# Second pair of each feed-forward entry on two other banks; conv layer norm, merged tiles and heads' taps in another order around the weight splits

## What is computed

```
mod = silu(c) @ ada_w + ada_b                     # 9 vectors of 1024: shift, scale, gate x3
h = modulate(rms_norm(x)); g, u = split(h @ w_in) # w_in 1024 x 5632
x += 0.5 * g1 * ((silu(g) * u) @ w_out)           # feed-forward 1, inner width 2816
h = modulate(rms_norm(x)); q,k,v,u,gates = split(h @ w_mix_in)   # 1024 x 7168
y_attn = rms_norm(diff_attention(q, k, v)) @ w_attn_branch       # 8 heads, 2 maps each
z = depthwise_conv31(a * sigmoid(g))              # causal, over tokens, from u
y_conv = silu(layer_norm(z)) @ w_conv_branch
x += g2 * ((sigmoid(ga) * y_attn + sigmoid(gb) * y_conv) @ w_mix_out)
x += 0.5 * g3 * feed_forward_2(modulate(rms_norm(x)))
```

## Time and profile before

| | |
|---|---|
| plain runs | 2654.38 us (2653.51 to 2656.37) |
| the profiled execution | 2656.59 us |
| its span, first to last instruction | 2654.8 us |
| mean granted TensorE clock | 0.992 |
| TensorE matmul / weight load busy | 2571.9 / 2064.5 us |
| VectorE / ScalarE / GpSimd busy | 1672.3 / 972.7 / 102.4 us |
| moved by DMA | 311.93 MB, mean 117 GB/s |

### The profile page before, as it was taken

One profiled execution on the slowest core, in us unless ns is written; L12 is line 12 of the kernel. 1 busy time (PEld: TensorE's weight loads), 2 busy tenths in 40 slices (PEclk: granted clock), 3 DMA queues, 4 the chain that ended last, 5 costly groups with the idle time before them and its releaser, 6 DMA issues.

```text
span 2654.8 us, 34931 instructions
## 1 busy us (share of the span) xinstructions
PE 2571.9 (97%) x11578; PEld 2064.5 (78%) x11578; DVE 1672.3 (63%) x2449; ACT 972.7 (37%) x1637; POOL 102.4 (4%) x163
## 2 busy tenths in 40 slices
PE   4899999999999999999999999999999999999998
PEld 2688888777777887888878888877777778788886
DVE  3655576789888666543365555679888866644333
ACT  2422222554454433222232222244554453432222
POOL 0000001000000000000000000101000000000000
PEclk9899999999999999999999999999999999999998
DMA  6355456222223344543325555632222333333332
GB/s 225 114 157 158 150 182 220 77 81 82 79 83 88 92 126 118 153 125 92 102 84 157 156 154 164 222 99 84 79 83 79 91 92 90 87 95 95 95 98 92
DMA packets 469951, 311.93 MB, mean 117 GB/s; under 512 B 11047, under 2 KB 447529, under 8 KB 468872
## 3 DMA queue, kind: packets, MB, share of 16 engines
q1 hardware_dynamic: 445260, 227.69, 29.3%
q0 software_dynamic: 19584, 75.51, 8.4%
q10 hardware_dynamic: 5052, 8.02, 1.0%
HBM read 306.13 MB, written 5.05 MB: 117 GB/s over the span
## 4 chain that ended last, share of the span: by engine, by line
PE 79%; DVE 8%; issue 8%; ACT 3%; ACTq 1%; DVEq 0%
PE bank L1211 24%; PE bank L1213 23%; PE bank L1212 23%; DVE conv_part L1004 3%; PE bank L1406 1%; ACT w_hi L394 1%; ACTq L446 1%; PE bank L1237 1%; DVE w_lo L683 1%; PE bank L1232 1%; PE bank L1233 1%; PE bank L1283 1%; DVE scaled L705 1%; PE bank L1377 1%; PE bank L1310 1%
## 5 line engine op out<-in xcount | busy, mean ns | idle before, releaser
L683 DVE TENSOR_TENSOR w_lo<-w_raw,w_hi 128x1024 fp32r<-128x1024 f32 (+1 forms) x434 | 522.4, 1204 | 626.4 <-ACT w_hi L394 625.7
L1211 PE MATMUL bank<-h_hi,w_hi 128*128 128x512 f32 x2112 | 842.1, 399 | 14.9 <-DVE scaled L908 10.3
L1213 PE MATMUL bank<-h_hi,w_lo 128*128 128x512 f32 x2112 | 826.1, 391 | 0.0
L1212 PE MATMUL bank<-h_lo,w_hi 128*128 128x512 f32 x2112 | 824.6, 390 | 0.0
L394 ACT ACTIVATE w_hi<-w_raw 128x1024 fp32r<-128x1024 f32 (+1 forms) x434 | 451.6, 1041 | 862.9 <-PE bank L1213 851.5
L1211 PEld LDWEIGHTS bank<-h_hi,w_hi 128*128 128x128 f32 x2112 | 398.2, 189 | 109.0 <-issue 28.0
L1213 PEld LDWEIGHTS bank<-h_hi,w_lo 128*128 128x128 f32 x2112 | 397.7, 188 | 85.0
L1212 PEld LDWEIGHTS bank<-h_lo,w_hi 128*128 128x128 f32 x2112 | 398.7, 189 | 78.6 <-issue 0.5
L1004 DVE SCALAR_TENSOR_TENSOR conv_part<-glu,conv_taps,conv_part 128x512 f32<-128x512 f32 x464 | 318.6, 743 | 0.0
L1211 PE MATMUL bank<-s_hi,w_hi 128*128 128x512 f32 x704 | 274.6, 390 | 0.0
L1213 PE MATMUL bank<-s_hi,w_lo 128*128 128x512 f32 x704 | 274.0, 389 | 0.0
(11 more groups left out here) (182 smaller groups left out, 2647.1 us busy)
## 6 DMA issues: line engine op xcount, KB each, us to landing
w_raw<-in_ffn_w_in SPq DMA_DIRECT2D x176, 512.0 KB, 3.8
ada_raw<-in_ada_w POOLq DMA_DIRECT2D x128, 512.0 KB, 4.8
w_raw<-in_w_mix_in SPq DMA_DIRECT2D x112, 512.0 KB, 3.7
w_raw<-in_ffn_w_out SPq DMA_DIRECT2D x64, 512.0 KB, 3.8
w_raw<-in_ffn_w_out SPq DMA_DIRECT2D x32, 384.0 KB, 3.4
w_raw<-in_w_mix_out SPq DMA_DIRECT2D x18, 512.0 KB, 3.8
ada_first<-in_ada_w POOLq DMA_DIRECT2D x8, 1024.0 KB, 24.4
w_raw<-in_w_attn_branch SPq DMA_DIRECT2D x16, 512.0 KB, 3.8
```

The costliest lines, as they stand in the source:

```text
L683: dve.tensor_tensor(wlo[slot][:, 0:n, :], raw[slot][:, 0:n, :], whi[slot][:, 0:n, :].bitcast(F32), ALU.subtract).then_inc(w_lo[slot], 1)
L1211: pe.matmul(acc, wh, hi[:, k0 + k, :], start=first and k == 0, stop=False)
L1212: pe.matmul(acc, wh, lo[:, k0 + k, :], start=False, stop=False)
L1213: mm = pe.matmul(acc, wl, hi[:, k0 + k, :], start=False, stop=last and k == n - 1)
```

## The change

Three parts.

**Entries.** The second pair of each feed-forward entry (tile 1) accumulates into banks TP[0] and TP[1] (banks 4 and 5, used by the heads for turned matrices) and no longer waits for a reader of its bank; ScalarE and VectorE read tile 1 there. TensorE's tile 2, now written out ahead of the loop (`PEELED` 3), needs one read of G less.

**Heads and order.** The taps between the splits are dealt out differently. In "ab" and "brb" VectorE's tile work comes ahead of the split of the next weights and waits for the product itself.

**Layer norm.** The mean moves to block 1 of the next slab, the variance to block 1 of slot 0 of the second ab pair. Squares, centring and sums are spread differently over the slots; the root stands behind one more split on ScalarE, the reciprocal one slot later on VectorE.

```diff
-PEELED = 2
+PEELED = 3
-LN_SQUARES = {(2, 1): (0, 1), (3, 0): (2, 3), (3, 1): (4, 5, 6, 7)}
+LN_SQUARES = {(3, 0): (0, 1, 2, 3), (3, 1): (4, 5), (4, 0): (6, 7)}
...
-                    act.activation(T[0][:, :], G[0][:, :], ACT.Tanh, scale=0.5).then_inc(sem("g_tanh"), 1)
+                    act.activation(T[0][:, :], gate[:, :], ACT.Tanh, scale=0.5).then_inc(sem("g_tanh"), 1)
...
-                ffn_tile(1, False)
+                ffn_tile(1, False, TP[0])
...
                     conv_norm(j, 0)
+                    w_hi_part(p + 1, 1)
                     if j == LN_VAR:
                         root(l * AUXN + AUX_VAR, l * UNITS + UNIT_LN)
-                    w_hi_part(p + 1, 1)
...
-                assert PEELED == 2
-                ffn_tile(1, split=False)
+                assert PEELED == 3
+                ffn_tile(1, split=False, banks=TP)
+                ffn_tile(2)
...
-                    conv(8, 17)
+                    conv(8, 16)
                     if not first:
                         w_lo_part(p + 1, 1)
-                    conv(17, 22)
+                    conv(16, 21)
                     w_lo_part(p + 2, 0)
-                    conv(22, 25)
+                    conv(21, 23)
                     dve.wait_ge(sem("bt_in"), (hh + 1) * 16)
                     scores(3)
                     if not first:
                         head_lo(hh - 1, tile(AOLO2, h - 1), tile(AOHI2, h - 1))
-                    conv(25, 26)
+                    conv(23, 26)
                     scores(2)
...
                     for t in range(2):
-                        w_lo_part(p + 1, t)
                         if j >= KT // 2:
                             n = 2 * (j - KT // 2) + t
+                            dve.wait_ge(w_used[t], p + 1)
                             dve.scalar_tensor_tensor(out=GA[:, n, :], in0=GA[:, n, :], scalar=1.0, in1=G[t][:, :],
                                                      op0=ALU.add, op1=ALU.mult).then_inc(acc_read[t], 1)
+                        w_lo_part(p + 1, t)
...
                             add_ln(3)
-                        if (j, t) == (LN_MEAN + 1, 1):
                             centre(4)
                             centre(5)
+                        if (j, t) == (LN_MEAN + 1, 1):
                             add_ln(4)
                             centre(6)
                             add_ln(5)
                             centre(7)
+                        if (j, t) == (LN_VAR, 0):
                             add_ln(6)
                             add_ln(7)
-                        if (j, t) == (LN_VAR, 0):
+                        if (j, t) == (LN_VAR, 1):
                             reciprocal(l * AUXN + AUX_VAR, l * RSN + RS_VAR)
...
-                        w_lo_part(l * PAIRS + PAIR0["brb"] + i + 1, t)
+                        dve.wait_ge(w_used[t], l * PAIRS + PAIR0["brb"] + i + 1)
...
                         dve.tensor_tensor(F[t][:, :], tile(GA2, j), T[t][:, :], ALU.add).then_inc(sem("merged"), 1)
+                        w_lo_part(l * PAIRS + PAIR0["brb"] + i + 1, t)
                         dve.wait_ge(sem("m_hi"), l * KT + j + 1)
...
-                        pe.wait_ge(acc_read[slot], use)
+                        if banks is G:
+                            pe.wait_ge(acc_read[slot], use)
...
+                    wh, wl, acc = whi[slot][:, n, :], wlo[slot][:, n, :], banks[slot][:, :]
...
-            two_slabs(pair + 1, use + 1, lambda j: pe.wait_ge(sem("unit_lo"), l * UNITS + UNIT_NORM[k] + j + 1))
+            two_slabs(pair + 1, use + 1, lambda j: pe.wait_ge(sem("unit_lo"), l * UNITS + UNIT_NORM[k] + j + 1),
+                      banks=G if name == "mix" else TP)
...
-                def ffn_tile(i):
+                def ffn_tile(i, reads=0):
                     p = l * PAIRS + PAIR0[n_in] + i
-                    u = l * USES + USE0[n_in] + i
+                    u = l * USES + USE0[n_in] + i - reads
...
                 entry(l, 2 * w, n_in)
+                ffn_tile(2, reads=1)
...
-                branch("gb", LN_MEAN + 1, HHI, HLO, ({7: conv_mean}, {}))
+                branch("gb", LN_MEAN + 1, HHI, HLO, ({}, {1: conv_mean}))
...
-                branch("ab", 0, AOHI, AOLO, ({}, {3: conv_variance}))
-                with pe.Fori(1, KT // 2) as i:
+                branch("ab", 0, AOHI, AOLO)
+                branch("ab", 1, AOHI, AOLO, ({1: conv_variance}, {}))
+                with pe.Fori(2, KT // 2) as i:
                     branch("ab", i, AOHI, AOLO)
```

More of the change, by code:

```diff
@@ L502, in _, with ffn_tile @@
                 act.activation(SHI[:, 0, :], F[0][:, :], ACT.Copy).then_inc(sem("s_hi"), 1)
-                def ffn_tile(i, split=True):
+                def ffn_tile(i, split=True, gate=G[0]):
                     p = l * PAIRS + PAIR0[n_in] + i
@@ L898, in _, with ffn_tile @@
                 dve.tensor_tensor(SLO[:, 0, :], F[0][:, :], SHI[:, 0, :].bitcast(F32), ALU.subtract).then_inc(sem("s_lo"), 1)
-                def ffn_tile(i, seq=0, steps=(), split=True):
+                def ffn_tile(i, seq=0, steps=(), split=True, banks=G):
                     p = l * PAIRS + PAIR0[n_in] + i
@@ L906, in ffn_tile @@
                     dve.wait_ge(acc_read[1], u)
-                    dve.scalar_tensor_tensor(out=T[1][:, :], in0=T[0][:, :], scalar=1.0, in1=G[0][:, :],
+                    dve.scalar_tensor_tensor(out=T[1][:, :], in0=T[0][:, :], scalar=1.0, in1=banks[0][:, :],
                                              op0=ALU.add, op1=ALU.mult).then_inc(acc_read[0], 1)
@@ L915, in ffn_tile @@
                     dve.wait_ge(sem("s_lo"), (l * 2 + w) * FT + i)
-                    dve.tensor_tensor(F[0][:, :], G[1][:, :], T[1][:, :], ALU.mult).then_inc(acc_read[1], 1)
+                    dve.tensor_tensor(F[0][:, :], banks[1][:, :], T[1][:, :], ALU.mult).then_inc(acc_read[1], 1)
                     dve.wait_ge(sem("s_hi"), (l * 2 + w) * FT + i + 1)
@@ L1214, in slab, with two_slabs @@
             mm.then_inc(w_used[slot], 1)
-        def two_slabs(pair, use, ready, shift=None, at={}):
+        def two_slabs(pair, use, ready, shift=None, at={}, banks=G):
             lag = 4
@@ L1227, in two_slabs @@
                         pe.wait_ge(w_lo[slot], pair + 1)
-                        pe.wait_ge(acc_read[slot], use)
+                        if banks is G:
+                            pe.wait_ge(acc_read[slot], use)
                     if slot == 0:
                         ready(n)
-                    wh, wl, acc = whi[slot][:, n, :], wlo[slot][:, n, :], G[slot][:, :]
+                    wh, wl, acc = whi[slot][:, n, :], wlo[slot][:, n, :], banks[slot][:, :]
                     pe.matmul(acc, wh, HHI[:, n, :], start=n == 0, stop=False)
```

## The result

The changed kernel takes 2619.75 us (2619.12 to 2620.49, 4 runs) against 2654.19 us before (2653.51 to 2656.37, 4 runs): ratio 0.9869, 95% interval 0.9852 to 0.9886. Forecast: 2620.1 us. Profiled execution against profiled execution it is 2620.49 against 2656.59 us, 36.1 us, where the sum had 34.3. The closeness of 0.35 us is in part luck: the sum is 1.8 us too small, and the profiled execution lies 0.7 us above the median now, not 2.2 us, which takes 1.5 us back.

A forecast was written before the change was run, and what follows sets the result against it. TensorE, busy 97% of the span, bounds the kernel, so only its waits and slow clock can give time. Terms sum to 34.3 us off 2656.59 us profiled: 2622.3 us profiled, 2620.1 us plain median; range 2614 to 2632 us.

The forecast's parts named there:

- Entries: Feed-forward entries: tile 2 stops waiting for VectorE's gate read; split weights are late next; 2.74 us each, 10.95 us in all.
- Heads: Head loop, 12 passes: waits for split weights (6.3 us gained) and row maxima (3.0 us) go, no new wait.
- Layer norm: Conv layer norm: moving the mean gains 1.3 us and the variance 4.6 us; a new wait costs 1.6 us.
- rival A: Entries: something in the entry itself, not the wait, lowers the clock; 8.0 us of gain missing, 2628 us; chance 0.13.
- Clock: Behind four entry waits and one variance wait: half-rate falls follow idles of 2.3 to 2.6 us; 6.3 and 1.7 us gained.
- the new wait: Attention branch, third pair: split weights late behind the reciprocal, 0.8 us in each layer, -1.6 us in sum.
- Merged tiles: Conv branch: tile work moves into VectorE's idle before each split; last merged tile's wait goes, 1.7 us gained.
- What I costed at nothing: Peeled tile and leftover entry waits taken as 0 (bounds up to 0.5 us an entry); no new heads wait.
- B: Entries, heads, conv stage: terms set to 0 come out at their bounds as new waits; 2630 us; chance 0.15.
- D: Entries and heads: another equally long wait behind the gate read, new head waits; only some 10 us gained, 2644 us; chance 0.05.
- rival C: Branch stages: VectorE late with 32 splits now behind tile work; slower, 7 us lost, 2661 us; chance 0.05.
- The signs of being wrong: TensorE idle over 8 us between 110 and 2630 us, or the clock at 0.5 anywhere in it.

## Why the prediction was right

**Entries.** The step held to 0.02 us: what is late next is the split weights, and they come just in time, with nothing to spare. Against rival A, the clock falls go when the wait goes and come back with it. What the prediction said for A, that the fall starts about 1 us after the wait has ended, was read off one entry: behind the wait that ends at 1016.75 the first matmul already takes 0.56 us to the next, so there the fall had begun.

**Clock.** The mechanism held and the count was wrong. I read five falls behind six waits as nearly sure; it is about two in three behind an idle of 2.3 to 2.6 us (27 of 44). The profiled execution before was one with many. That fits that the profiles differ by 36.1 us and the medians by 34.4: plain runs of the kernel before with a mean clock of 0.994 took 2653.0 to 2655.1 us, those with 0.992 took 2656.5 to 2657.4, about two falls more by an estimate from 1.6 us each (three with 0.993 took 2656.0 to 2658.2). It is not shown: where the falls lay in the plain runs is not on record, and the start-up varies as much.

**Heads.** Right in both terms and in what comes next; 1.0 us too small together with the mean. The wait for split weights also costs its first matmul: after an idle of 0.70 us at 569.74 the next one starts at 570.04, 0.30 us later and not 0.23. In the changed kernel it is 0.23 us (565.76 to 565.99). About 0.08 us at each of the 12 split waits is the 1.0 us that the sum had left out. It isn't the idle as such that costs this: at the entries the first matmul takes 0.31 us before the change and after it (109.47 to 109.78, with no idle), so there nothing of it was gained.

**Layer norm.** The mean and the variance came as worked out; the new wait is 0.31 us of idle (0.54 us in all) and not 0.8, its place right. The chain from the start of the reciprocal to the end of that split took 14.13 us. The smaller wait, twice, is 0.5 of the 0.8 us by which this stage beat the sum.

**Merged tiles.** Right, 2.0 us for 1.7; 0.2 of the rest is the first matmul, which took 0.34 us to the next behind either wait (946.80 to 947.14).

**What I costed at nothing.** The first head of layer 1 lost 0.4 us. The wait for its second weights is 0.66 us, not 0.27. VectorE's score step there starts 0.37 us late with nothing that the profile shows before it:

```profile
499.33 0.42 DVE L1042 CUSTOM_DVE_ANT_0 probs<-bank,bias_tile 128x256 f32<-128x256 f32 x1 [0.37 <-issue]
```

Every kernel here with the peeled tile has that 0.66 us wait, and none without it; in layer 2 no kernel has it. What in the longer program does it was not tried.

**Rivals B to D.** No margin that I took for 0 opened, but for this one, so B and D did not come. Nor did rival C's lateness: the conv branch is as long as before to 0.01 us.

**The signs of being wrong.** Taken by the letter both are met: between 110 us and the end TensorE is idle for 18 us, and the clock is at 0.50 from 2601.3 to 2611.3. The limit of 2630 us was set on the old kernel's axis; the changed kernel reaches its last norm, which no part of the change touches, some 35 us earlier. From 110 to 2590 us the idle is 4.5 us and no fall lies there.

## What to carry to other kernels

Before a wait is removed, read what is late next, on the same engine's line, and move that too: one half of the heads' change was worth nothing alone and the other 3.1 us, the whole 11.5 us. When a wait of TensorE is 1.8 us or longer its price can be more than its length; count half-rate matmuls behind it, and count them in several executions, since they do not come every time. Work that only reads a finished bank fits into the wait of a split for another engine: put ahead of the split it gained 1.1 us in each attention branch and 1.0 us behind each conv branch here.

## What the runs showed of the hardware

An idle of 1.8 us, with TensorE busy on both sides, let the granted clock fall to 0.5 (the 1.2 GHz level) in 2 of 4 cases, and one of 2.6 us left it at full rate in 10 of 28. The Trainium skill (TensorE: Matmul & The Clock Gate, "HAM oscillation — how this bites in real kernels") asks for longer gaps than these; here the measured falls decide, and a shorter idle is no protection. The Trainium skill (the same page, "What's actually happening") says that the number of slow matmuls at a kernel's start varies between runs of the same kernel; here the mean clock of one kernel's plain runs varies too, from 0.992 to 0.994, though that start is only one part of it. An idle of 0.41 us had no fall behind it in 4 cases, one of 0.72 to 0.87 us none in 12. The kernel before spreads over 3 to 5 us in each set of runs, the changed one, with no fall in the body of its profile, over 1.4 us; that the falls make the difference is likely and not shown.
